# Seven half-block products instead of eight in three up groups of a feed-forward

## The reference, cut to what matters

```
u = rms_norm(h, g_mlp) @ w_ff1          # (512 x 1024) @ (1024 x 4096)
h = h + jnp.square(jax.nn.relu(u)) @ w_ff2   # (512 x 4096) @ (4096 x 1024)
```

## Time and profile before

| | |
|---|---|
| median of 3 runs | 2062.11 us (2060.41 to 2064.62) |
| profiled execution, span from first to last instruction | 2057.3 us |
| what a run has beside the span (median less span) | 4.8 us |
| TensorE busy | 2013.4 us, 98% of the span |
| TensorE matmuls | 10,148 |
| matmuls in the chain that ended last | 88% of the span |

### The profile page before, as it was taken

One profiled execution on the slowest core, in us unless ns is written; L12 is line 12 of the kernel. 1 busy time (PEld: TensorE's weight loads), 2 busy tenths in 40 slices (PEclk: granted clock), 3 DMA queues, 4 the chain that ended last, 5 costly groups with the idle time before them and its releaser, 6 DMA issues.

```text
span 2057.3 us, 26250 instructions
## 1 busy us (share of the span) xinstructions
PE 2013.4 (98%) x10148; PEld 1574.5 (77%) x10148; DVE 1135.5 (55%) x2020; ACT 867.9 (42%) x1381; POOL 917.4 (45%) x1157
## 2 busy tenths in 40 slices
PE   6999999999999999999999999999999999999998
PEld 2877676888888767768888888786776788888877
DVE  5366758988393579955522231466996543222235
ACT  4542434443233556784322222445578532222242
POOL 1344205876566325541555555302355155555540
PEclk9999999999999999999999999999999999999999
DMA  9034631322323211103333323322111332332331
GB/s 328 25 108 143 217 123 50 105 94 80 121 84 102 89 42 42 62 21 123 92 103 103 99 86 103 102 69 83 42 42 42 103 97 98 103 103 83 102 102 62
DMA packets 188299, 194.26 MB, mean 94 GB/s; under 512 B 8592, under 2 KB 184080, under 8 KB 187792
## 3 DMA queue, kind: packets, MB, share of 16 engines
q1 hardware_dynamic: 187600, 189.44, 28.5%
q10 hardware_dynamic: 576, 3.15, 0.4%
HBM read 190.48 MB, written 2.10 MB: 94 GB/s over the span
## 4 chain that ended last, share of the span: by engine, by line
PE 88%; DVE 6%; POOL 2%; ACT 2%; DMA 1%; issue 1%; SPq 0%; DVEq 0%; ACTq 0%; POOLq 0%
PE ps L808 20%; PE ps L810 20%; PE ps L809 20%; PE ps L827 3%; PE ps L829 3%; PE ps L828 3%; PE ps L855 2%; POOL wl L2900 1%; DVE mix L2512 1%; PE ps L844 1%; PE ps L845 1%; PE ps L846 1%; PE ps L1355 1%; PE ps L1428 1%; PE ps L1411 1%; PE ps L1374 1%
## 5 line engine op out<-in xcount | busy, mean ns | idle before, releaser
L2900 POOL TENSOR_TENSOR wl<-ring,wh 128x256 fp32r<-128x256 f32 x1008 | 754.2, 783 | 807.5 <-ACT wh L1465 807.2
L1465 ACT ACTIVATE wh<-ring 128x1024 fp32r<-128x1024 f32 (+1 forms) x298 | 309.0, 1044 | 311.1 <-PE ps L810 256.9
L808 PE MATMUL ps<-xh,wh 128*128 128x512 f32 (+1 forms) x976 | 383.1, 393 | 2.6 <-POOL wl L2900 2.6
L810 PE MATMUL ps<-xh,wl 128*128 128x512 f32 (+1 forms) x976 | 380.6, 390 | 0.0
L809 PE MATMUL ps<-xl,wh 128*128 128x512 f32 (+1 forms) x976 | 380.6, 390 | 0.0
L808 PE MATMUL ps<-acts,wh 128*128 128x512 f32 x880 | 343.5, 390 | 0.7 <-POOL wl L2900 0.4
L810 PE MATMUL ps<-acts,wl 128*128 128x512 f32 x880 | 342.4, 389 | 0.0
L809 PE MATMUL ps<-acts,wh 128*128 128x512 f32 x880 | 342.4, 389 | 0.0
L2512 DVE SCALAR_TENSOR_TENSOR mix<-ps,par,mix 128x441 f32<-128x441 f32 (+2 forms) x352 | 213.7, 687 | 29.3 <-ACT mix L1712 29.3
L808 PEld LDWEIGHTS ps<-xh,wh 128*128 128x128 f32 (+1 forms) x976 | 183.0, 188 | 47.0 <-issue 9.1
L810 PEld LDWEIGHTS ps<-xh,wl 128*128 128x128 f32 (+1 forms) x976 | 183.0, 187 | 39.4
(11 more groups left out here) (443 smaller groups left out, 3031.4 us busy)
## 6 DMA issues: line engine op xcount, KB each, us to landing
ring<-in_w_ff_dram SPq DMA_DIRECT2D x64, 1024.0 KB, 5.2
ring<-in_w_in_dram SPq DMA_DIRECT2D x28, 1024.0 KB, 5.0
ring<-in_ffn_w_up_dram SPq DMA_DIRECT2D x22, 1024.0 KB, 4.9
ring<-in_w_ada_dram SPq DMA_DIRECT2D x17, 1024.0 KB, 5.0
ring<-in_w_out_dram SPq DMA_DIRECT2D x12, 1024.0 KB, 5.1
ring<-in_ffn_w_down_dram SPq DMA_DIRECT2D x8, 1024.0 KB, 5.0
ring<-in_w_ple_gate_dram SPq DMA_DIRECT2D x8, 1024.0 KB, 5.0
early<-in_w_ada_dram SPq DMA_DIRECT2D x7, 1024.0 KB, 10.8
```

What stands on the lines that cost most here:

```text
L808: t.matmul(b[0:m, 0:n], s.hi[:, k, a:a + m], x2[0][:, k, :], start=k == ks[0], stop=False)
L810: i = t.matmul(b[0:m, 0:n], s.lo[:, k, a:a + m], x2[0][:, k, :], start=False, stop=k == ks[-1])
L1465: a.activation(s.hi[:, :, c], s.ap[:, :, c], ACT.Copy).then_inc(*up("hi", "hi", name, hf))
L2900: i = p.tensor_tensor(s.lo[:, k:k + 2, c], s.ap[:, k:k + 2, c], s.hi[:, k:k + 2, c].bitcast(F32), ALU.subtract)
```

## The change

Groups 1, 2 and 3 of the up projection (weight columns 1,024 to 4,095) are no longer made of plain products. For each weight tile the 1,024 x 256 weights are seen as 2x2 blocks (512 rows x 128 columns each), and x as 2x2 blocks (512 features x 256 tokens each). The 2x2 block product, eight half-block products, is made with seven, by sums of blocks on both sides:

- The weights of those groups are laid out so that a tile holds its four blocks ("quarters" of 128x512) side by side, loaded by one transfer of the same 1 MB. VectorE makes three weight sums for each tile (`sums`, four instructions of 128x512, in the ring slot and in one extra buffer `two`).
- Seven parts of 128x512 are split for each tile: ScalarE the high parts; of the low parts five on GpSimd (two instructions of 128x256 each) and two on VectorE (one of 128x512 each). `wh` and `wl` become eight places of 128x512.
- TensorE does seven products for each tile, each of 12 matmuls with 256 tokens, into four half-filled or filled PSUM banks. Four banks instead of two are used for each tile.
- The results are put together: ScalarE copies half of the first bank (`n.copied`), VectorE adds (three instructions of 128x512 and one of 128x256, each with a PSUM operand), then does relu and scale as two instructions from SBUF to SBUF; the squares are as before.
- The sums of blocks of x are made during up 0 (`turned`): 16 VectorE instructions of 128x256, one of 128x1024, four ScalarE copies of 128x1024 and four VectorE subtractions of 128x1024.
- The order of the groups stays: up 0, up 1, down 0, up 2, down 1, up 3, down 2, down 3. The load of `p` on ScalarE's queue moves from behind up 0 to ahead of down 2.

The core of the diff (`seven` on TensorE, ScalarE and VectorE, the sums, and the low parts):

```diff
+SEVEN_RAW = (0, 1, None, 0, 1, 3, 2)
+SEVEN_X = ((0, 0), (1, 0), 1, 2, (1, 1), 3, 0)
+SEVEN_BANK = ((0, 0), (1, 0), (1, 1), (2, 0), (2, 1), (3, 0), (3, 1))
+SEVEN_WHO = ("pool", "vec", "pool", "pool", "vec", "pool", "pool")
+SEVEN_SUMS = (2, 3, 4)
+SEVEN_SUM_OF = {2: 2, 3: 3, 4: 4, 6: 2}
...
+        for (name, hf), n in when.items():
+            if self.named[name].seven and hf in SEVEN_SUMS:
+                soon = first[name] < n
+                self.sum_at.setdefault(self.uses[n - soon][0], ([], []))[soon].append((name, hf))
...
+                def seven(g, i):
+                    name = ("ff1", l, g, i)
+                    s = W.named[name]
+                    for p in range(7):
+                        (q, u), x, bank = SEVEN_BANK[p], SEVEN_X[p], (*name, "bank", SEVEN_BANK[p][0])
+                        use((*name, p), name, (p,), who="pool")
+                        if u == 0:
+                            take(bank, keep=True, where=None)
+                        b = ps(bank)[:, 256 * u:256 * u + 256]
+                        e.wait_ge(*at("lo", name, p))
...
+                        for k in range(4):
+                            hi, lo = [y[:, 128 * k:128 * k + 128] for y in (s.hi[p], s.lo[p])]
+                            t.matmul(b, hi, x2[0][:, k, :], start=k == 0, stop=False)
+                            t.matmul(b, hi, x2[1][:, k, :], start=False, stop=False)
+                            j = t.matmul(b, lo, x2[0][:, k, :], start=False, stop=k == 3)
...
             def high_half(name, hf):
...
+                for b in W.before[name, hf]:
+                    e.wait_ge(*over(W.through[b][0]))
+                if s.seven and hf in SEVEN_SUM_OF:
+                    e.wait_ge(*at("sum", name, SEVEN_SUM_OF[hf]))
+                a.activation(s.high[hf], s.raw[hf], ACT.Copy).then_inc(*up("hi", "hi", name, hf))
...
+                def seven(g, i):
+                    name = ("ff1", l, g, i)
+                    for p in range(7):
+                        high((*name, p))
+                        if p == 0:
...
+                            out_of((*name, "bank", 0), n.copied, ps((*name, "bank", 0))[:, 0:256])
+                    for u in range(2):
+                        j = i + 4 * u
+                        e.wait_ge(*at("relu", l, g, j))
...
+                        a.activation(n.U[g % 2][0][:, j, :], n.uu[2 * (i % 2) + u], ACT.Square).then_inc(*up("act", "u2h", l, g, j))
...
             def low(key):
 
+                now_, soon = W.sum_at.get(key, ((), ()))
+                for name, p in now_:
+                    sums(name, p)
                 for name, hf in W.split_at.get(key, ()):
                     if W.half_at[name, hf] == "vec":
                         low_half(name, hf)
+                for name, p in soon:
+                    sums(name, p)
...
+            def sums(name, p):
+
+                s = W.named[name]
+                q = s.quarter
+                if p == 2:
+                    e.wait_ge(*at("load", name))
+                    v.tensor_tensor(q[2], q[2], q[3], ALU.add).then_inc(*up("vec"))
+                    if name in W.seven_before:
+                        e.wait_ge(*at("lo", W.seven_before[name], 2))
+                    after()
+                    v.tensor_tensor(s.raw[2], q[2], q[0], ALU.subtract).then_inc(*up("vec", "sum", name, 2))
+                elif p == 3:
+                    e.wait_ge(*at("lo", name, 0))
+                    after()
+                    v.tensor_tensor(q[0], q[3], s.raw[2], ALU.subtract).then_inc(*up("vec", "sum", name, 3))
+                else:
+                    e.wait_ge(*at("lo", name, 1))
+                    after()
+                    v.tensor_tensor(q[1], q[1], s.raw[2], ALU.subtract).then_inc(*up("vec", "sum", name, 4))
...
+                def turned(jl):
+                    if jl in (2, 3):
+                        for j in (0, 1) if jl == 2 else (2, 3):
...
+                            v.tensor_scalar(first, h1, gj, None, ALU.mult).then_inc(*up("vec"))
+                            after()
+                            v.scalar_tensor_tensor(four[0], h2, gj, first, ALU.mult, ALU.subtract).then_inc(*up("vec", "sum", l, 0))
+                            after()
+                            v.scalar_tensor_tensor(four[1], h4, gk, four[0], ALU.mult, ALU.subtract).then_inc(*up("vec", "sum", l, 1))
+                            after()
+                            v.scalar_tensor_tensor(four[3], h3, gk, four[1], ALU.mult, ALU.subtract).then_inc(*up("vec", "sum", l, 3))
+                    elif jl >= 4:
+                        if jl == 4:
+                            v.tensor_tensor(n.plain[3], n.plain[2], n.plain[0], ALU.subtract).then_inc(*up("vec", "sum", l, 2))
+                        x = jl - 4
+                        e.wait_ge(*at("sumh", l, x))
+                        v.tensor_tensor(n.sums[x][1], n.plain[x + 1], n.sums[x][0].bitcast(F32),
+                                        ALU.subtract).then_inc(*up("vec", "suml", l, x))
...
+                    for p in range(7):
+                        low((*name, p))
+                        if p == 2:
+                            e.wait_ge(*taken((*name, "bank", 0)))
+                            v.tensor_tensor(two(ua), two(bank(1)), twice(n.copied), ALU.add).then_inc(*free((*name, "bank", 1)))
+                        elif p == 4:
+                            b = bank(2)
+                            e.wait_ge(*taken((*name, "bank", 1)))
+                            v.tensor_tensor(two(n.third), two(b), twice(ua[:, 256:512]), ALU.add).then_inc(*free((*name, "bank", 2)))
+                        elif p == 6:
+                            b = bank(3)
+                            e.wait_ge(*taken((*name, "bank", 2)))
+                            v.tensor_tensor(two(ub), two(b), twice(n.third[:, 0:256]), ALU.add).then_inc(*up("vec"))
+                            v.tensor_tensor(ua[:, 256:512], b[:, 256:512], n.third[:, 256:512], ALU.add).then_inc(*free((*name, "bank", 3)))
+                            e.wait_ge(*taken((*name, "bank", 3)))
+                            for u, x in enumerate((ua, ub)):
+                                v.scalar_tensor_tensor(x, x, 0.0, n.rs2, ALU.max, ALU.mult).then_inc(*up("vec", "relu", l, g, i + 4 * u))
+                    for u, x in enumerate((ua, ub)):
+                        square_low(g, i + 4 * u, x)
...
+                for k in range(2 if s.seven else s.kt // 2):
+                    lo, raw, hi = [x[:, 256 * k:256 * k + 256] if s.seven else x[:, 2 * k:2 * k + 2, :]
+                                   for x in (s.low[hf], s.raw[hf], s.high[hf])]
+                    i = p.tensor_tensor(lo, raw, hi.bitcast(F32), ALU.subtract)
```

More of the change, by code:

```diff
@@ L325, in restart, with add @@
         self.uses = []
-    def add(self, name, src, kt, w, split=True, own=False):
+    def add(self, name, src, kt, w, split=True, own=False, seven=False):
         t = Tile(len(self.tiles), src if type(src) is list else [src], kt, w, split, own)
-        t.at, t.name = self.n_split % 2, name
-        self.n_split += split
+        t.name, t.seven = name, seven
+        if seven:
+            t.parts = 7
+        n = 8 if seven else 4 * split
+        t.places = [(self.place + i) % 8 for i in range(n)] if split else [self.place % 8]
+        self.place += n
         self.tiles.append(t)
         self.named[name] = t
-    def columns(self, name, hf):
-        return slice(128 * hf, 128 * hf + min(128, self.named[name].w - 128 * hf))
     def plan(self):
-        self.split_at, self.half_at, self.before, self.through = {}, {}, {}, {}
-        order, held, done_raw = [], {}, {}
+        self.split_at, self.half_at, self.before, self.through, self.sum_at = {}, {}, {}, {}, {}
+        order, held, done_raw, first, when = [], {}, {}, {}, {}
         for n, (key, name, halves, over, ahead, who) in enumerate(self.uses):
@@ L414, in build @@
         wh_t, wl_t = sb("wh", 2 * SLOT, F32R), sb("wl", 2 * SLOT, F32R)
+        with ExitStack() as low:
+            sb("beside", 2048, where=low)
+            sum3 = sb("sum3", 2048, F32R, where=low)
         mix_t, ring = sb("mix", 4096), sb("ring", NSLOT * SLOT)
@@ L560, in build @@
             with ExitStack() as low:
+                with ExitStack() as high:
+                    sum0 = sb(f"sum0{l}", 2048, F32R, where=high)
                 cut = Cut(sb(f"arena_f{l}", 3072, where=low), 3072)
@@ L565, in build @@
                     a1 = sb(f"acts{l}1", 8192, F32R, where=high)
+                    sum1, sum2 = [sb(f"sum{i}{l}", 2048, F32R, where=high) for i in (1, 2)]
+                with ExitStack() as high:
+                    plain = sb(f"plain{l}", 5120, where=high)
                 with ExitStack() as high:
@@ new lines, in down @@
+                def down(g, j):
+                    product(("ff2", l, g, j), ("ff2", l, g, j // 2), j % 2, n.U[g % 2], xk=("u2", l, g), who="pool")
+                    if g == 3 and j == 4:
```

(20 more changed lines are left out.)

267 lines of the change are left out of this document (146 added, 121 removed).

## The result

The changed kernel takes 2114.81 us (median of 4 runs, 2113.77 to 2118.81), the kernel before 2061.26 us beside it on the same chip. The ratio is 1.0271, with a 95% interval of 1.0256 to 1.0286: **2.7% slower**, some 54 us. The prediction said 2102 us with a range of 2045 to 2140.

What follows compares the result with a forecast made beforehand. VectorE with its port waits on GpSimd sets the pace of the seven groups: 16 + 2 + 2 = 20 us a layer, 40 for two, takes 2057.3 to 2097, with 4.8 between span and median 2102; range 2045 to 2140.

Steps and rivals of the forecast that it cites:

- TensorE's gain: Seven-product up tiles: 9.9 us each on TensorE instead of 10.9, 24 us less over 24 tiles if TensorE stays the bound.
- TensorE stays the bound: Rival for the seven-product groups: GpSimd's bursts fall into VectorE's PSUM instructions and waits; 2038 to 2050 us, chance 0.16.
- VectorE's cycle: VectorE's time per seven-product tile: 10.1 us undisturbed, 14.0 with eight of 12 two-SBUF-input instructions meeting GpSimd at 0.49 each.
- A later group: Second and third seven-product group of a layer: 45.6 us against 43.6 before, +2.0 each.
- The waits at the end: Two short waits closing a seven-product group, for part 6's high part and the first down half: 2.0 us together.
- T: VectorE's cycle for one seven-product tile: 14.0 us, bounds 10.1 to 16.0; counted twice in a group.
- The first group: Up 1 of each layer: sums of x in VectorE's up 0 backlog make it 14 us later, +16 with the +2.
- Costed at nothing: ScalarE's work, weight loads, PSUM banks and the moved load of p in the changed groups: no added time.
- the granted clock: Clock rival: waits in every group halve TensorE's clock, up to 5.7 us more each, about 2136 us; chance 0.12.
- The signs: Seven groups: VectorE over 90% busy, squares and sums 1.1 to 1.25 us, longest wait over 5 us at up 1's part 4.
- The 4.8 us "beside the span": Whole kernel: 4.8 us between profiled span and median, added to 2097 to give 2102.
- The upper bound: All instructions meet GpSimd: first group +26, the others +6, 38 us a layer, 2139 us.

Runs made afterwards that it cites:

- the other order: Against the changed kernel, each seven-product tile is followed at once by two down products of the group before: 2069.97 us.

## Why the prediction was right, step by step

- *TensorE's gain.* 24 us were predicted if TensorE stays the bound. Where nothing else bounds it a tile takes 10.1 us, not 9.9: the step is 0.120 us, and the weight loads are busy for 40.33 of 40.40 us in the run with narrow GpSimd instructions. So 19 us are there to be had, and the old order gets none of them.
- *VectorE's cycle.* Predicted 14.0 us with eight of twelve instructions meeting GpSimd; measured 13.69, and eight are long. The mechanism was right, the closeness of the number is partly luck. Undisturbed 10.1 was predicted and 10.63 measured in the run with narrow GpSimd instructions; a meeting was put at 0.49 us and cost 0.38 on average. The two errors cancel. The count of eight was a choice between none and twelve, and the meetings fall on other instructions than forecast: low parts, sums, relus and the second subtraction are long, the squares stay at 0.68 to 0.69.
- *A later group.* Predicted 45.6 us (+2.0), measured 48.2 (+4.7). VectorE reached part 1 of the last tile at 31.1 us after the start (31.5 predicted). Then part 2 began at 37.5, 6.4 us later instead of 4.5: all three VectorE instructions of that stretch meet GpSimd, 3.4 us instead of 1.95, and GpSimd's two take 2.1. The waits at the end came to 2.9, not 2.0. **These two terms are what was mis-sized,** 2.8 us in a group. In the same sum the meetings had been counted for T and left out of the chain behind it.
- *The first group.* VectorE's low part of part 1 of the second tile was predicted at 1029.0 and started at 1028.20. The prediction put the whole delay into one wait at part 4 of the first tile. That is wrong in place: TensorE waited 3.2 us in front of the last product of up 0, 2.3 in front of up 1's first part, and 1.3 and 1.6 in front of parts 3 and 4 of the first tile. ScalarE goes in order, and its high parts stood behind squares whose relus VectorE hadn't made.

```profile
1009.46 0.47 PE L865 MATMUL ps<-xh,wh 128*128 128x512 f32 x1 [3.24 <-POOL wl L3069]
...
1024.72 0.36 PE L1305 MATMUL ps<-sum,wh 128*128 128x256 f32 x1 [1.25 <-issue]
...
1027.94 0.39 PE L1305 MATMUL ps<-xh,wh 128*128 128x256 f32 x1 [1.56 <-DVE wl L2108]
```

  The amount, 18.6 us with up 0, is near the 16 predicted. The run with early sums shows that the instructions of the sums make 9 of it.
- *Costed at nothing.* Loads and banks showed no wait. ScalarE wasn't the bound, but its order passes VectorE's lateness on, and it took over at once when its share grew.
- *Rivals.* That TensorE stays the bound is excluded (42.4 busy in 48.2 us); it does become true with narrow GpSimd instructions and in the other order. Within the feed-forwards the granted clock did fall, but only around the waits of up 0 and up 1. In layer 0 it was 0.58 from 1017.4 to 1021.4, behind the waits of 3.2 and 2.3 us:

```profile
1017.40:1021.40 4.00, 3.97 (x21) 4.00 (x22) 3.27 (x6) 2.36 (x4) 1.75 (x2) 0.58 0.02 4
```

  In layer 1 it was 0.50 from 1715 to 1721, in the last product of up 0 behind its wait of 3.2 us, and 0.54 from 1731 to 1737. In the later groups, with waits of up to 1.4 us, it stayed at 1.00. By the mean over up 1 of layer 0 (0.97) TensorE lost some 2 us to it, but the time shows next to nothing: right behind it TensorE waits for part 3, whose low part came through VectorE and ScalarE, and in the run with narrow sums of x, up 1 of layer 0 takes 56.1 us at a clock of 1.00. The prediction also says that the trace of before shows such a fall once; it shows two more (0.66 in 740 to 745 and in 1420 to 1425).

- *The signs.* VectorE was to be busy for over 90% and is at 90% in a later group. A group was to span some 45 us and the first some 60; measured 48.2 and 56.2. The wait of over 5 us at part 4 didn't come.

In sum the prediction is 8 us short in each layer, 5.4 of them in the two later groups and 2.6 in the first with up 0: 40 us were added for both layers, and the span grew by 56.7. That 2102 comes as near as 13 us to 2115 is luck in one more term. The 4.8 us "beside the span" were the median of several runs less the span of one profiled execution. An execution takes only 1.8 us more than its own span (2115.82 for 2114.0), so the profiled one was some 3 us faster than that median, and for the changed kernel median less span is 0.8. So 4 of the 17 us are covered by that. The upper bound adds up to 2138, not 2139.

## What to carry to other kernels

Work taken from the bound engine is worth what the next engine leaves of it: count the added instructions of every other engine for the same tile, with their steps, and add a wait for each VectorE instruction with both inputs in SBUF that can meet GpSimd, however short it is. When an engine is over its budget in one stretch and idle in the next, interleave the stretches before taking work away; here the order alone was worth 45 us. And a wait put down to the last engine of a chain (GpSimd here) says little about which one is late: follow it back until an engine without idle time is found.

## What the runs showed of the hardware

- A VectorE instruction with both inputs in SBUF that meets GpSimd mostly takes 0.35 to 0.55 us longer, whatever its width: 8 columns took 0.17 to 0.23 us alone and 0.65 to 0.71 with GpSimd at work, 512 columns 0.69 and 1.04 to 1.23. The relu from SBUF does so too (0.69 and 1.05 mean), and so does a scale from one SBUF tensor (L2683, 256 columns: 0.34 and 0.83). The Trainium skill, "SBUF — State Buffer", section Who interferes with whom, names both kinds and an exclusive hold for the whole instruction; the extra time that doesn't depend on VectorE's own width agrees with it.
- GpSimd pays as well: its instruction of 128x256 takes 0.74 us at the median over the changed kernel and 0.99 to 1.09 on average in up 2.
- With 256 columns the loads of 128x128 weights fill the time of TensorE (40.33 of 40.40 us), and the step is 0.120 us where 0.118 had been measured near the start of the kernel before.
